# First pair's rows by one-hot products, the two choices summed in quarters, and products without a reader in two waits

## The reference, cut to what matters

```python
def _hmoe(h, ...):
    gsel = argmax(h @ rg_w + rg_b)             # best of 4 groups
    el_sel = (h @ re_w + re_b)[gsel]           # its 4 experts
    top_v, top_i = top_k(el_sel, 2)            # two choices for each token
    top_w = softmax(top_v) * gprob
    hid = silu(h @ wg[e]) * (h @ wu[e])        # 1024 -> 256, expert e of 16
    return sum over the 2 choices of top_w * (hid @ wd[e])
...
y = _hmoe(h, ...)
x = _layer_norm(ALPHA * x + gt2 * y, ln_g, ln_b)
```

## Time and profile before

| what | value |
|---|---|
| median of three runs | 1056.74 us (1055.49 to 1057.18) |
| profiled execution: its own time | 1059.74 us |
| profiled execution: its span | 1057.9 us |
| mean granted TensorE clock | 0.924 |
| busy: TensorE, its weight loads, VectorE, ScalarE, GpSimd | 884.6, 601.0, 332.2, 230.8, 150.1 us |
| moved by DMA | 230.41 MB, 218 GB/s on average |

### The profile page before, as it was taken

The page is one execution under the profiler, slowest core; times in us unless marked ns, Lnnn a source line. Parts: engine busy times, 40 slices in busy tenths (PEclk is TensorE's granted clock), DMA queues, the critical chain, the costliest instruction groups (busy, mean ns, idle before and its releaser), DMA issues.

```text
span 1057.9 us, 18846 instructions
## 1 busy us (share of the span) xinstructions
PE 884.6 (84%) x8102; PEld 601.0 (57%) x8102; DVE 332.2 (31%) x849; ACT 230.8 (22%) x521; POOL 150.1 (14%) x200
## 2 busy tenths in 40 slices
PE   2799999889985698899883799898899989998834
PEld 0377667779774375655441467544467756554412
DVE  0513342535425436311113401222130363111134
ACT  0312225223220413111000313212132141110003
POOL 0100002011100024321112210000000143211122
PEclk9899989999998899899996799989899998998966
DMA  9732221340246553589975944546564735899831
GB/s 384 315 134 103 81 80 56 117 162 5 93 162 256 208 212 138 204 347 423 425 323 206 387 160 143 221 159 215 199 267 183 315 148 193 329 425 423 358 106 45
DMA packets 29057, 230.41 MB, mean 218 GB/s; under 512 B 6800, under 2 KB 7216, under 8 KB 13840
## 3 DMA queue, kind: packets, MB, share of 16 engines
q1 hardware_dynamic: 19200, 208.66, 49.3%
q0 software_dynamic: 8064, 15.82, 4.2%
q10 hardware_dynamic: 1712, 4.75, 1.3%
HBM read 223.21 MB, written 16.32 MB: 226 GB/s over the span
## 4 chain that ended last, share of the span: by engine, by line
PE 68%; DMA 18%; DVE 6%; issue 3%; ACT 3%; POOL 1%; SPq 1%; ACTq 0%; POOLq 0%; DVEq 0%
PE ps L638 21%; PE ps L975 9%; DMA arena<-in_w 8%; DMA arena<-in_experts 6%; PE ps L764 5%; PE ps L659 5%; PE ps L1022 4%; PE ps L620 4%; PE ps L771 3%; PE ps L1128 2%; PE ps L625 2%; DMA arena<-zbuf 2%; DMA ring<-in_w 2%; PE ps L910 1%; PE ps L777 1%
## 5 line engine op out<-in xcount | busy, mean ns | idle before, releaser
L638 PE MATMUL ps<-arena,ring 128*128 128x288 f32 x896 | 230.7, 419 | 15.9 <-ACT arena L1958 6.0
L638 PEld LDWEIGHTS ps<-arena,ring 128*128 128x128 f32 x896 | 172.4, 195 | 75.1 <-issue 20.7
L975 PE MATMUL ps<-arena 128*64 128x256 f32 x960 | 120.4, 405 | 20.6 <-DMA arena<-in_experts 12.1
L975 PEld LDWEIGHTS ps<-arena 128*64 128x64 f32 x960 | 76.8, 146 | 63.9 <-issue 20.4
L620 PE MATMUL ps<-con,arena 128*128 128x128 f32 (+3 forms) x398 | 68.8, 302 | 38.3 <-DVEq L1723 34.4
L620 PEld LDWEIGHTS ps<-con,arena 128*128 128x128 f32 (+3 forms) x398 | 49.0, 150 | 77.0 <-DVEq L1723 36.1
L659 PE MATMUL ps<-arena,csil 128*32 128x512 f32 x256 | 40.3, 760 | 39.6 <-DMA arena<-in_w 39.6
L764 PE MATMUL ps<-arena 64*64 64x64 f32 x1888 | 62.5, 219 | 5.0 <-issue 4.1
L764 PEld LDWEIGHTS ps<-arena 64*64 64x64 f32 x1888 | 59.3, 136 | 10.7 <-issue 9.0
L1022 PE MATMUL ps<-arena 128*64 128x512 f32 x208 | 58.4, 598 | 0.8 <-DVE arena L1664 0.8
L1987 ACT ACTIVATE arena<-ps 128x128 f32<-128x128 f32 x36 | 10.0, 277 | 198.3 <-PE ps L975 189.2
(11 more groups left out here) (300 smaller groups left out, 1170.7 us busy)
## 6 DMA issues: line engine op xcount, KB each, us to landing
arena<-in_experts SPq DMA_DIRECT2D x30, 2048.0 KB, 20.5
ring<-in_w SPq DMA_DIRECT2D x24, 2048.0 KB, 8.7
arena<-in_w SPq DMA_DIRECT2D x16, 2048.0 KB, 13.2
arena<-in_experts SPq DMA_DIRECT2D x30, 1024.0 KB, 17.1
ring<-in_experts SPq DMA_DIRECT2D x6, 2048.0 KB, 19.4
ring<-in_experts SPq DMA_DIRECT2D x6, 1024.0 KB, 16.2
arena<-in_lora SPq DMA_DIRECT2D x1, 2560.0 KB, 40.7
hbuf<-arena SPq DMA_DIRECT2D x4, 512.0 KB, 2.9
```

The source lines that it names most:

```text
L638: last = mm(ps[:, tile % 4, 0:T], wslot[j][:, k, o * P:(o + 1) * P], rhs_at(k), start=k == 0, stop=k == KT - 1)
L975: last = mm(ps[64 * j:64 * j + 64, 2 + b, 0:256], x(k), ewgu[slot][:, k, j * 256:(j + 1) * 256], start=k == 0, stop=k == KT - 1)
```

## The change

The first pair's rows no longer come from hbuf. While htok is still on chip, first_rows multiplies each block of 128 features of htok with the first 128 columns of SEL[0], block of tokens by block of tokens, which gives the turned rows of pair 0 straight in PSUM: 8 times 3 products instead of one gather and eight turns. It stands ahead of tables(0). step_t(1) moves from behind step_u(0) to behind step_h(0). GpSimd's order becomes fetch(1), fetch(2), places, fetch(3). xsel moves to the ring of weights. The spins ahead of the pair's rows shrink from 4 to 2, and the 3 behind tables(1) go. Ahead of the turning of the sum stand 24 new spins, and ahead of project(4) there are 5. VectorE adds the two choices in four quarters of 256 columns.

```diff
+GATHERS = (NPAIR // 2 - 1, NPAIR // 2)
...
-        xsel = [cut(at_rows + n * D, D) for n in range(2)]
-        xselT = [cut(at_rows + 2 * D, D), take(D)]
-        ysel = [take(D) for _ in range(2)]
+        ysel = [cut(at_rows + n * D, D) for n in range(2)]
+        xselT = [take(D) for _ in range(2)]
+        xsel = [ring[:, ECOL + n * D:ECOL + (n + 1) * D] for n in range(2)]
...
                 pe.wait_ge(s["ht_evac"], 6 * (layer + 1))
-                spin(2, 4)
+                spin(2, 2)
...
-                tables(0)
-                for i, n in enumerate(TOK):
-                    last = mm(ps[:, 7, 448:464], ones[0:n, :], mask[0:n, i, :], start=i == 0, stop=i == 2)
-                last.then_inc(s["cnt_mm"], 1)
-                tables(1)
...
+                def first_rows():
+
+                    for k in range(KT):
+                        for i, n in enumerate(TOK):
+                            last = mm(ps[:, k // 4, k % 4 * P:(k % 4 + 1) * P], htok[0:n, i, k * P:(k + 1) * P],
+                                      SEL[0][0:n, i * 4 * C:i * 4 * C + 2 * C], start=i == 0, stop=i == 2)
+                        if k % 4 == 3:
+                            last.then_inc(s["xt_mm"], 1)
+
                 def step_t(p):
 
-                    pe.wait_ge(s[f"gath{p % 2}"], 16 * ((p0 + p) // 2 + 1))
+                    pe.wait_ge(s[f"gath{p % 2}"], 16 * (layer * GATHERS[p % 2] + (p + 1) // 2))
...
-                spin(2, 3)
-                step_t(0)
+                pe.wait_ge(s["sel_ready"], 4 * layer + 1)
+                first_rows()
+                tables(0)
+                for i, n in enumerate(TOK):
+                    last = mm(ps[:, 7, 448:464], ones[0:n, :], mask[0:n, i, :], start=i == 0, stop=i == 2)
+                last.then_inc(s["cnt_mm"], 1)
+                tables(1)
                 for e in range(NE):
                     step_u(e)
                     if e < 2:
                         tables(2 + e)
                     if e:
                         step_h(e - 1)
-                    if e % 2 == 0:
+                    if e == 1:
+                        step_t(1)
+                    if e % 2 == 0 and e:
                         if e + 2 < NE:
                             step_t(e // 2 + 1)
-                        if e:
-                            step_d(e // 2 - 1)
+                        step_d(e // 2 - 1)
...
+                spin(6, 24)
                 for k in range(KT):
                     c = layer * KT + k
-                    if k % 4 == 0:
-                        pe.wait_ge(s["zsum"], 2 * layer + k // 4 + 1)
+                    if k % 2 == 0:
+                        pe.wait_ge(s["zsum"], 4 * layer + k // 2 + 1)
...
+            spin(6, 5)
             project(4, lambda k: X[:, k, :], ready=lambda k: pe.wait_ge(s["x_ready"], KT + k + 1), then=last_of_turn)
...
-                for h in range(2):
-                    c = slice(h * 512, (h + 1) * 512)
-                    dve.wait_ge(s[f"z_in{h}"], 48 * (layer + 1))
+                for q in range(4):
+                    c = slice(q * 256, (q + 1) * 256)
+                    dve.wait_ge(s[f"z_in{q // 2}"], 48 * (layer + 1))
...
                 def fetch(p):
                     pool.wait_ge(s["tbl_ready"], 4 * layer + p // 2 + 1)
-                    if p >= 2:
+                    if p > 2:
                         pool.wait_ge(s["xt_mm"], 2 * (p0 + p - 1))
...
-                for p in range(2):
+                for p in range(1, 3):
                     fetch(p)
                 places()
-                for p in range(2, 4):
-                    fetch(p)
+                fetch(3)
```

More of the change, by code:

```diff
@@ L2002, in moe @@
                     step_u(e)
-                    if e % 2 == 0 and e + 2 < NE:
+                    if e == 1:
+                        step_t(1)
+                    if e % 2 == 0 and 0 < e < NE - 2:
                         step_t(e // 2 + 1)
```

## The result

| | before | changed |
|---|---|---|
| median, same chip | 1056.96 us (1055.49 to 1060.88, 4 runs) | 1073.21 us (1070.56 to 1076.96, 4 runs) |
| ratio, 95% interval | | 1.0151 [1.0109, 1.0192] |
| the same pair once more | 1060.10 us (34 runs) | 1067.87 us (12 runs), 1.0073 [1.0041, 1.0105] |
| profiled execution: own time | 1059.7 us | 1070.56 us |
| span | 1057.9 us | 1069.1 us |

A forecast was written before the change was run, and what follows sets the result against it. TensorE holds 68% of the chain of waits, DMA 18%; transfers bound the weight stream. Entry 3.8, sum in quarters 1.2 and spins ahead of project(4) -0.7 give +4.3 us on the median 1056.7: 1061.0, range 1052.0 to 1066.0.

The forecast's parts named there:

- the first term of the sum: Entry into the experts: first_rows, tables and counts make step_u(0) start 1.3 us later a layer (bounds +1.1 and +2.0).
- The second term: Entry: step_u(0), right behind table products, runs mostly at 1.2 GHz, 5.36 us instead of 3.67: +1.7 a layer.
- The rival in which it keeps the full clock: Entry: step_u(0) stays at full clock despite first_rows and tables ahead of it; 3.4 us less, 1057.6; chance 0.17.
- the turn moved: Between step_u(0) and step_d(0): step_t(1) goes behind step_h(0), where TensorE idles, so one turn's 1.1 us comes off.
- Signals that come late: Behind step_h(0): step_u(2) would wait for ScalarE's late copies for pair 1, up to 3.3 us a layer, 1067.6; chance 0.12.
- The stream follows step_d(0): Expert weights: transfers bound the stage, so a later end of step_d(0) (+1.9 us a layer) moves its end one for one.
- The rival in which the later step_d(0) is hidden: Expert weights: the stream has slack elsewhere, so the later step_d(0) costs nothing; 3.8 us less, 1057.2; chance 0.10.
- The quarters: Sum of the choices on VectorE: 4.5 us instead of 3.9, so residual and squares start later: +0.6 a layer, +1.2.
- The 24 spins: Ahead of the turning of the sum: the clock falls before the squares anyway, which stay at 1.93 us a step: 0.
- the first rival: Norm behind the experts: the spins hold the clock at 2.4 GHz, a step takes 0.97 us, total 1051.2; chance 0.14.
- The 5 spins: Ahead of project(4): if the clock holds, at most 1.5 us gained; half taken, -0.7, in layer 0 alone.
- The two remaining rivals: Spins ahead of turning at 0.52 us a record: 1080, chance 0.02; first_rows at 12.3 us: 1071.6, chance 0.01.

The follow-up runs named there:

- The entry alone: Kernel before with only first rows by products, step_t(1) moved, gathers reordered and the old spins there cut; sum and later spins unchanged: 1068.82 us, ratio 1.0103.
- three delays by spins: Kernel before with 12 spins, 12 once more, and 24 spins ahead of the first step_d in each layer: 1067.32, 1067.29 and 1078.67 us.
- the changed kernel with the clock held: Changed kernel with 30 spins instead of 24 ahead of the turning and 6 more ahead of the first squares: 1065.16 us, 1.0073 against before.

## Why the prediction was wrong

The direction was right, the size was not: the forecast of 1061.0 and the range up to 1066.0 lie below both medians, 1073.21 and 1067.87. The step that failed is the first term of the sum, the start of step_u(0): +1.3 us a layer in the text, +3.4 in the runs. The second term, step_u(0) at the low clock, was too small as well.

**First rows: the term that was mis-sized.** The text took 7.0 us for 48 records and bounded them by 7.7. They took 8.51 in every profile of a kernel with the new entry, 0.177 us each, above the 0.16 of the nearest row with 128 columns. The mask products of attention have a constant for weights, and here each of the 24 products brings other weights; whether that is the reason was not tried. The second half of the error is tables(1), costed at 1.70 although had shown the clock at 0.62 right behind the table products: 2.94 and 2.16. From the start of select the forecast was 12.25 us to step_u(0), and it was 14.97 and 14.18. Over the ten layer passes of five profiles with the new entry as it is in the change it is 14.4, over the twelve of six profiles with the old entry and no delay 11.0: +3.4 a layer, where +1.3 was forecast.

**Step_u(0) at the low clock: right, and dearer.** Its 32 records took 5.50 and 6.41 us, forecast 5.3; over the ten passes it is 6.2, so +2.6 a layer where +1.7 was forecast. Two runs show where that comes from: without the old spins it takes 5.95 in the kernel before, and with the tables behind it, it keeps 3.67 and step_u(1) takes 5.36. The rival in which it keeps the full clock is thus real in mechanism, but it needs another order and gives nothing back.

**From step_u(0) to step_d(0): the turn moved.** Forecast +0.6 a layer (+1.7 - 1.1). Measured 20.7 against 19.6 us over the same passes: +1.1. The pause of 0.62 us in step_u(1) is gone, as held possible: 3.60 us, where it had lasted from 434.98 to 439.83. But the change didn't take it away. It took 4.85 and 5.13 us in the two layers of that one profile, and 3.67 in both layers of the nine other profiles with the old entry. Step_u(2), which the text kept at 5.36, took between 3.67 and 6.59 us in either entry. Signals that come late, a rival, did not show: ScalarE's copies for pair 1 started 0.64 us after the turns' start (447.34 and 447.98) where it had been 4.7, and step_u(2) waited 0.79 us for them. All told the entry costs about 4.5 us a layer where 1.9 was forecast, 9 in both. The entry alone measured +10.9.

**The stream follows step_d(0): right in the stages, less in the totals.** The down weights' issue moved from 35.4 to 39.4 us behind select, and step_d(0) to the sum is 124.3 us over the ten passes with the new entry, 124.0 over the twelve without. The rival in which the later step_d(0) is hidden fell: three delays by spins cost 5.8, 7.3 and 14.7 us. But they were 11.7, 11.7 and 23.3, so the totals pass on half to some three quarters (0.6 to 0.8 by the medians). By the same share the entry's 9 us would be worth some 5 to 7 in the total. Where the rest goes stays open.

**The quarters: the part in view right, the total open.** The residual starts 4.66 us behind the sum, forecast 4.5, and the first squares 0.7 later than with halves. Over the stretch from sum to mean, the four passes with quarters alone average 17.3 us, the sixteen with halves and without spins ahead of the turning 16.9, single ones from 14.5 to 19.1. That is 0.8 us for both layers, and the squares' start says 1.4. The two measurements of quarters alone say 2.5 to 8 together. That leaves both out, though the second one by itself (0.6 to 8.6) does not, and on top of the other parts nothing was found. What makes up the rest stays open.

**The 24 spins: right.** I had the first squares 8.7 us behind the last spin and the clock fallen by then. They came 8.7 us behind it (576.70 and 585.43), and the clock fell 5.2 us behind it, in the turning. Over the eight layer passes of the four profiles with 24 spins it fell 4.1 to 5.2 us behind the last spin, when TensorE had waited 3.3 to 4.8 us for the sum and was at most 1.5 us into the turning. It never lasted to the gap ahead of the squares. The result is the one forecast, squares at 1.93 a step and no gain in the total (with halves the stretch from sum to mean is 15.4 us over four passes with the spins and 16.9 over sixteen without, within the scatter of single ones). The gain of the first rival exists: with 32 spins that reach to 0.5 us before the turning, and three in the gap behind it, sum to mean is 12.95 us and the kernel 9.5 us faster than before. So the rival's mechanism holds. Its price of 9.8 us is near the total, in part by luck: a step took 1.08 us and not 0.97, and project(4) gained nothing where the text had 0.8. The two stretches alone show 8.5 us against the profile of before and 7.9 against the mean of 16.9. What 24 spins lacked was work for TensorE in the waits behind them, the one ahead of the turning first. Whether filling that one alone would do was not tried.

**The 5 spins: the term was nothing, and the open question stays open.** I took half of a possible 1.5, on the condition that the clock holds. It didn't: the spins moved its fall from the wait into the records, and they ran at 0.50 for some 3.4 us, where it had been 3.8. The first 16 records took 5.8 to 6.3 us in the six profiles with the five spins and 5.8 to 6.6 in the others. What they would cost with the clock up all the way no run shows. (The text's excess of 1.9 us is 2.1 over the 3.88 that it names.)

**The two remaining rivals.** The spins ran at full speed (11.91 us for 48 records), not at 0.52 a record. First rows took 8.51 and not 12.3, so the product at four turns did not come true: 0.354 us a product over a turn of 0.13 is 2.7. The Trainium skill ("TensorE: Matmul & The Clock Gate", Terms) says that the transpose mode is four times faster for float32. By that a product would take an estimated 0.52 us; the measured 0.354 lies between it and my row's 0.32, and nearer to the row.

**The spread.** The three times shown before the change lay within 1.7 us, and I read them as the spread of the kernel. In the first set of experiments 29 executions of it went from 1047.98 to 1074.27 us, the middle one at 1057.26. The stage from project(4) to the mean of layer 1, which no experiment touches, took 248.04 us at a mean clock of 0.94 in the profile of before. Over all sixteen profiles it took from 243.40 at 0.96 (five spins alone) to 259.44 at 0.88 (the changed kernel with the clock held). So a profile of one execution carries some 10 us that have nothing to do with an edit, and the range should have been wider on that side. It also limits what is shown here: 1.0151 and 1.0073 are one effect measured twice. The stages give some +10 us (9 for the entry, 0.8 to 1.4 for the quarters), or 1.01, which lies between the two. With the entry at 5 to 7 us it would be 6 to 8, and the repeat's 7.7 is in that. Why the first measurement came out at 16 stays open; it has four runs a side, of a kernel whose single executions spread over 26 us.

## What to carry to other kernels

Before a wait is filled with real products in place of spins, look at what stands ahead of the next long step: here the granted clock fell behind the products with 6 and 16 columns, and six records without a reader had been hiding that. Spins that are to hold the clock must reach into every wait up to the work that they are for: 24 of them with 3.3 to 4.8 us of waiting behind them left the squares at the lower clock, while 32, with three more in the next gap, held it and gave 0.9%. Where a run is to show what a step costs with the clock up, look whether it was up during the step itself, and not only ahead of it; with the five spins it was not. Price a product from a row of the same columns with the same traffic of weights, and check a kernel's spread in an untouched stage before a change of 4 us is argued over. Average over every profile that bears on a stage: the pause in step_u(1) stood in the one profile that the forecast was read from, and in none of nine others.

## What was unexpected in the hardware

A float32 product record with 128 columns and new 128 by 128 weights took 0.177 us, one with 6 columns 0.142 (1.70 for 12), one of the spins with 288 columns 0.24 (3.88 for 16), all at the full clock. A record with one twenty-first of the columns of another cost four fifths of it.

TensorE, busy without a break according to its records, was granted 0.50 from 432 to 438, behind products of six columns. The cost falls on whatever stands next, and in different sizes: a step_u about the entry that the low clock met took 4.97 to 6.66 us instead of 3.67, eight turns 1.97 instead of 1.09.

Over the 29 executions of the kernel before, the time follows the mean granted clock with a correlation of -0.91: 8.3 us for each 0.01, from 1074.27 us at 0.903 to 1047.98 at 0.924. An untouched stage of 248 us went from 243 to 259 with its clock, as much as the larger of the two measurements of the whole change.
